# Last perceptron's second product by a seven-product scheme in groups 0 to 2, with weight sums made by adding transfers

## The reference, cut to what matters

```python
def sqrelu_mlp(h, w1, w2):
    a = jax.nn.relu(h @ w1)
    return (a * a) @ w2
```

## Time and profile before

| | us |
|---|---|
| runs, median of 3 | 2924.24 |
| runs, lowest and highest | 2922.78, 2925.26 |
| profiled execution, span from first to last instruction | 2926.7 |
| of it TensorE busy | 2837.7 |
| VectorE busy | 1374.1 |
| ScalarE busy | 1144.5 |
| GpSimd busy | 1320.1 |

### The profile page before, as it was taken

How to read it: one execution, slowest core, us unless ns; L and a number is a source line. 1 busy time by engine, 2 the same in 40 slices (tenths; PEclk the granted TensorE clock), 3 DMA queues, 4 the chain that set the end, 5 groups by cost and what they waited for, 6 DMA issues and landing times.

```text
span 2926.7 us, 41107 instructions
## 1 busy us (share of the span) xinstructions
PE 2837.7 (97%) x16278; PEld 2342.1 (80%) x16278; DVE 1374.1 (47%) x2568; ACT 1144.5 (39%) x1955; POOL 1320.1 (45%) x851
## 2 busy tenths in 40 slices
PE   7789999999999999989999999999999999999999
PEld 7577778888888786778888787888878878888887
DVE  4448653141121476632111467776543468667432
ACT  4353554453332443543322444332433543323332
POOL 4253247874444441344444553344534633435344
PEclk9999999999999999999999999999999999999999
DMA  6834114553223324032333332111222421212223
GB/s 242 318 113 142 51 44 146 180 165 100 94 94 130 110 82 156 1 108 87 96 99 94 111 113 70 58 58 58 87 72 87 137 88 47 66 58 73 87 72 115
DMA packets 84862, 300.69 MB, mean 103 GB/s; under 512 B 9536, under 2 KB 9920, under 8 KB 84288
## 3 DMA queue, kind: packets, MB, share of 16 engines
q1 hardware_dynamic: 84672, 298.07, 31.5%
HBM read 295.94 MB, written 2.10 MB: 102 GB/s over the span
## 4 chain that ended last, share of the span: by engine, by line
PE 84%; DVE 10%; ACT 2%; issue 2%; DMA 1%; POOL 1%; SPq 0%; POOLq 0%; ACTq 0%; DVEq 0%
PE ps L639 65%; PE ps L612 5%; DVE ps L2438 4%; PE ps L814 3%; PE ps L835 2%; PE ps L667 1%; PE ps L1011 1%; PE ps L1074 1%; PE ps L1085 1%; PE ps L939 1%; DMA t<-in_wmod 1%; PE ps L1252 1%; DVE t L2738 1%; DVE t L2776 1%; PE ps L952 0%
## 5 line engine op out<-in xcount | busy, mean ns | idle before, releaser
L639 PE MATMUL ps<-t,t 128*128 128x512 f32 (+3 forms) x9936 | 2218.6, 381 | 22.0 <-DVE t L2140 7.3
L639 PEld LDWEIGHTS ps<-t,t 128*128 128x128 f32 x9936 | 1781.0, 189 | 368.7 <-issue 35.5
L3087 POOL TENSOR_TENSOR t<-t,t 128x1024 fp32r<-128x1024 f32 (+3 forms) x464 | 1082.3, 2337 | 1078.8 <-ACT t L1397 1040.3
L1397 ACT ACTIVATE t<-t 128x1024 fp32r<-128x1024 f32 (+3 forms) x464 | 476.5, 1031 | 840.8 <-PE ps L639 784.9
L612 PE MATMUL ps<-t,t 128*128 128x128 f32 (+2 forms) x1662 | 238.4, 278 | 25.8 <-DVE t L2347 3.9
L612 PEld LDWEIGHTS ps<-t,t 128*128 128x128 f32 (+2 forms) x1662 | 190.1, 141 | 72.8 <-ACT t L1546 16.6
L2541 DVE TENSOR_TENSOR ps<-ps,t 128x512 f32<-128x512 f32 (+1 forms) x96 | 57.3, 606 | 343.7 <-ACT t L1739 343.7
L2558 DVE TENSOR_TENSOR t<-ps,t 128x512 f32<-128x512 f32 x56 | 38.2, 692 | 201.0 <-PE ps L639 200.9
L2438 DVE SCALAR_TENSOR_TENSOR ps<-t,t,ps 128x512 f32<-128x512 f32 (+1 forms) x174 | 116.1, 667 | 6.4 <-ACT ps L1654 0.6
L3107 POOL TENSOR_TENSOR t<-t,t 128x4 f32<-128x4 f32 (+2 forms) x96 | 86.4, 900 | 59.8 <-DVE t L2144 27.4
L814 PE MATMUL ps<-t,t 96*128 96x384 f32 (+1 forms) x320 | 104.6, 449 | 4.8 <-DVE t L2301 2.4
(11 more groups left out here) (279 smaller groups left out, 2480.3 us busy)
## 6 DMA issues: line engine op xcount, KB each, us to landing
t<-in_wbig SPq DMA_DIRECT2D x424, 512.0 KB, 3.5
t<-in_wmod SPq DMA_DIRECT2D x96, 512.0 KB, 6.6
t<-in_wbig SPq DMA_DIRECT2D x16, 416.0 KB, 3.1
t<-in_wbig SPq DMA_DIRECT2D x16, 332.0 KB, 2.9
t<-in_wbig SPq DMA_DIRECT2D x14, 256.0 KB, 2.6
t<-in_wbig SPq DMA_DIRECT2D x6, 384.0 KB, 3.1
t<-in_x SPq DMA_DIRECT2D x1, 2048.0 KB, 7.7
out<-t SPq DMA_DIRECT2D x8, 256.0 KB, 4.4
```

The lines of the kernel that those rows point to most:

```text
L639: m = p.matmul(out, lhs, rhs, start=kk == 0 and n == 0, stop=kk == tiles - 1 and n == 2)
L1397: a.activation(c.hi(w), c.raw(w), ACT.Copy).then_inc(w_hi.h, w_hi.up(("cut", w)))
L3087: g.tensor_tensor(c.lo(w), c.raw(w), c.hi(w).bitcast(F32), ALU.subtract).then_inc(w_lo.h, w_lo.up(("cut", w)))
```

## The change

In groups 0 to 2 of "ml1" the second product is made by seven products of quarter size in place of eight. Let the hidden activations of a group be a 2 x 2 of blocks A (256 tokens by 512 hidden columns) and w2's part a 2 x 2 of blocks W (512 by 512). The seven products are named 11, T3, 21, T4, T1, T2 and 22, in this order. Each has two units of 12 matmuls: two weight tiles, two banks of 128 tokens, three matmuls. T4, T2 and 22 accumulate in the banks of T3, 11 and T1, after VectorE has added those to Y.

Three of the weight operands are blocks of w2 (11, 21, 22). The other four are sums of two or three blocks. SyncE loads the first block of each into a buffer of its own (WN, 1 MB, `fetch_first`). GpSimd then issues five transfers that add into these buffers (`add`, `accum_op`): T3 += 22, T1 += 11, T4 += 22, T2 += T3 and T4 += T1, the last two from SBUF. They are issued in the first "w1" stage of a group (in group 0 in the second), behind GpSimd's cut of its unit 0 (one), unit 1 (two) and unit 2 (two).

The squares of the relu are kept in full in a buffer HF, with no split of their own. VectorE makes the four block sums of them (`full`) and all low parts (`low`); ScalarE makes the high parts (`part`). Of the 14 weight units of a group VectorE makes the low part where `by_vector` says so, GpSimd of the rest. VectorE adds each finished product to the places of Y that it belongs to (`took`, nine operations of 128x1024 in a group). Of the second output half, -Y is kept up to group 2, so group 3 subtracts. The row of gains moves behind product T1 of group 0.

The diff, cut to its core:

```diff
        "kc": [(3592, 4104)], "vc": [(4104, 4616)], "zc": [(4616, 5128)]}
+WN = ("11", "T3", "21", "T4", "T1", "T2", "22")
+WN_BLOCKS = ("11", "21", "22", "12")
+WN_SUM = {"T3": ("12", "22"), "T1": ("12", "11"), "T4": ("21", "22", "T1"), "T2": ("11", "T3")}
+WN_ADD = (("T3", 1), ("T1", 1), ("T4", 1), ("T2", 1), ("T4", 2))
+WN_PAIR = {"11": 0, "T3": 1, "21": 2, "T4": 1, "T1": 3, "T2": 0, "22": 3}
+WN_ONTO = {"T4": "T3", "T2": "11", "22": "T1"}
+WN_PART = {"11": 0, "T3": 1, "21": 2, "T4": 3, "T1": 0, "T2": 1, "22": 2}
 LAYER = {"c0": 0, "l0": 0, "c1": 1, "l1": 1, "mc0": 0, "ml0": 0, "ml1": 1}
+
+
+def seven(n, g):
+
+    return n == "ml1" and g < 3
 
...
                     block(("w1", n, g, h), "w_mlp_in", (i,), row, 4, [(1024 * g + 512 * h, 1024 * g + 512 * h + 512)])
+            if seven(n, g):
+                for name in WN_BLOCKS:
+                    row, col = 1024 * g + 512 * (int(name[0]) - 1), 512 * (int(name[1]) - 1)
+                    block(("wn", n, g, name), "w_mlp_out", (i,), row, 4, [(col, col + 512)])
+                continue
...
+    def wn_from(self, x):
+
+        return self.WN[x[1]][x[3]][:, x[4], :]
...
+    def by_vector(self, x):
+
+        if isinstance(x, tuple):
+            return x[4] == 1
+        key = self.units[x][0]
+        return key[0] == "wn" and key[3] != "11" and self.of[key].index(x) == 1
+
+    def seven_units(self, n, g, name):
+
+        return [("wn", n, g, name, r) for r in range(2)] if name in WN_SUM else self.of[("wn", n, g, name)]
...
+        self.WN, self.HF = {}, {}
+        w, a = self.row(one, [[128, 2, 1024]] * 3)
+        self.WN["ml1"] = dict(zip(WN_SUM, [*w, self.XC]))
+        self.HF["ml1"], _ = self.row(self.top - 16384, [[128, 4, 512]] * 2)
+
...
+        def seven_products(g):
+            for name in WN_SUM:
+                c.use(("r", (n, g, name)))
+            for name in WN:
+                at, onto = pairs[WN_PAIR[name]], WN_ONTO.get(name)
+                if onto:
+                    P.wait_ge(dve, ("took", n, g, onto))
+                else:
+                    for m in (at, at + 1):
+                        opened(m, ((dve, ("took", n, g, {0: "T2", 1: "T4", 2: "21", 3: "22"}[WN_PAIR[name]])),))
+                c.where[("wn", n, g, name)] = at
+                P.wait_ge(act, ("parth", n, g, name))
+                P.wait_ge(dve, ("partl", n, g, name))
+                aH, aL = c.wn_part(n, name)
+                for r, x in enumerate(c.seven_units(n, g, name)):
+                    c.use(("p" if name in WN_SUM else "w", x))
+                    hi, lo = (w.rearrange("p (k n) -> p k n", k=2) for w in (c.hi(x), c.lo(x)))
+                    P.wait_ge(w_hi, ("cut", x))
+                    P.wait_ge(dve if c.by_vector(x) else w_lo, ("cut", x))
+                    for k in range(2):
+                        for b in range(2):
+                            for m_, (wp, ap) in enumerate(((hi, aH), (hi, aL), (lo, aH))):
+                                m = p.matmul(c.BK[at + b], ap[:, 2 * r + k, 128 * b:128 * b + 128], wp[:, k, :],
+                                             start=not onto and r == k == m_ == 0, stop=r == k == 1 and m_ == 2,
+                                             skip_group_check=bool(onto))
+                        if k:
+                            m.then_inc(gemm.h, gemm.up(("w", x), *([("product", n, g, name)] if r else [])))
+                        yield
+                if (g, name) == (0, "T1"):
+                    row_of(n, i, 1, int(n[1] == "c"), pairs[2])
+            pairs[0:3] = pairs[2], pairs[1], pairs[0]
+
         for g in range(4):
...
+        while upto[0] < len(c.cut) and c.spos[c.cut[upto[0]]] <= c.spos[u] + ahead:
             w = c.cut[upto[0]]
             upto[0] += 1
             if c.before_in_slot(w) is not None:
                 A.wait_ge(gemm, ("w", c.before_in_slot(w)))
+            if isinstance(w, tuple):
+                A.wait_ge(c.s_sum[w[3]], ("sum", *w[1:4]))
+                a.activation(c.hi(w), c.wn_from(w), ACT.Copy).then_inc(w_hi.h, w_hi.up(("cut", w)))
+                continue
...
+        def part(g, name):
+            if name in ("11", "21", "T4"):
+                for kk in range(4 * int(name != "11"), 4 * int(name != "11") + 4):
+                    A.wait_ge(dve, ("hf", n, g, kk))
+            else:
+                A.wait_ge(dve, ("full", n, g, name))
+            if name in ("T1", "T2", "22"):
+                A.wait_ge(gemm, ("product", n, g, {"T1": "11", "T2": "T3", "22": "21"}[name]))
+            elif g:
+                A.wait_ge(gemm, ("product", n, g - 1, {"11": "T1", "T3": "T2", "21": "22", "T4": "T4"}[name]))
+            a.activation(c.wn_part(n, name)[0], c.wn_full(n, name), ACT.Copy).then_inc(
+                act.h, act.up(("parth", n, g, name)))
+
+        def first_parts(g):
+            yield
+            for name in ("11", "T3"):
+                part(g, name)
+                yield
+
+        def seven_products(g):
+            at = {0: ("21", "T4"), 2: ("T1",), 4: ("T2",), 6: ("22",)}
+            for m, x in enumerate(x for name in WN for x in c.seven_units(n, g, name)):
+                cut(x)
+                for name in at.get(m, ()):
+                    part(g, name)
+                if (g, m) == (0, 11):
+                    row_of(n)
+                yield
+                yield
+
         for g in range(4):
             for h in range(2):
-                main = product_gemm(("w1", n, g, h), 4, 8, lambda b: relu(g, h, b))
...
+        def low(g, name):
+            V.wait_ge(act, ("parth", n, g, name))
+            hi, lo = c.wn_part(n, name)
+            v.tensor_tensor(lo, c.wn_full(n, name), hi.bitcast(F32), ALU.subtract).then_inc(
+                dve.h, dve.up(("partl", n, g, name)))
+
+        def full(g, name):
+            F0, F1 = c.HF[n]
+            A11, A21, A12, A22 = F0[:, :, 0:256], F0[:, :, 256:512], F1[:, :, 0:256], F1[:, :, 256:512]
+            V.wait_ge(dve, dve.n)
+            out, one, other, op = {"T3": (A12, A11, A21, ALU.subtract), "T1": (A21, A21, A22, ALU.subtract),
+                                   "T2": (A11, A21, A11, ALU.subtract), "22": (A12, A12, A11, ALU.add)}[name]
+            v.tensor_tensor(out, one, other, op).then_inc(dve.h, dve.up(("full", n, g, name)))
...
+        def seven_products(g):
+            low(g, "21")
+            low(g, "T4")
+            cut(g, "T3")
+            yield from steps(4)
+            full(g, "T1")
+            full(g, "T2")
+            took(g, "11")
+            cut(g, "21")
+            yield from steps(4)
+            low(g, "T1")
+            full(g, "22")
+            took(g, "T3")
+            yield from steps(4)
+            low(g, "T2")
+            cut(g, "T4")
+            took(g, "21")
+            yield from steps(4)
+            low(g, "22")
+            cut(g, "T1")
+            took(g, "T4")
+            yield from steps(4)
+            cut(g, "T2")
+            took(g, "T1")
+            cut(g, "22")
+            yield from steps(4)
+            took(g, "T2")
+            yield from steps(4)
+            took(g, "22")
...
-        while upto[0] < len(c.cut) and c.pos[c.cut[upto[0]]] <= c.pos[u] + ahead:
+        while upto[0] < len(c.cut) and c.spos[c.cut[upto[0]]] <= c.spos[u] + ahead:
             w = c.cut[upto[0]]
             upto[0] += 1
+            if c.by_vector(w):
+                continue
+            if isinstance(w, tuple):
+                G.wait_ge(w_hi, ("cut", w))
+                g.tensor_tensor(c.lo(w), c.wn_from(w), c.hi(w).bitcast(F32), ALU.subtract).then_inc(
+                    w_lo.h, w_lo.up(("cut", w)))
+                continue
             G.wait_ge(w_hi, ("cut", w))
             G.wait_ge(c.s_of(w), ("raw", w))
...
+        def add(gr, name, step):
+            block = WN_SUM[name][step]
+            if step == 1:
+                G.wait_ge(c.s_wn[name], ("first", n, gr, name))
+            else:
+                G.wait_ge(c.s_sum[name], ("added", n, gr, name, step - 1))
+            if block in WN_SUM:
+                G.wait_ge(c.s_sum[block], ("sum", n, gr, block))
+                source = c.WN[n][block][:, :, :]
+            else:
+                source = c.wn_block(n, gr, block)
+            done = ("sum", n, gr, name) if step == len(WN_SUM[name]) - 1 else ("added", n, gr, name, step)
+            g.dma_start(c.WN[n][name][:, :, :], source, accum_op=ALU.add).then_inc(
+                c.s_sum[name].h, c.s_sum[name].landed(done))
+
+        def adds(gr):
+            for name, step in WN_ADD:
+                yield
+                yield
+                add(gr, name, step)
+
         for gr in range(4):
...
+    def fetch_first(n, g, name):
+        if g == 0:
+            S.wait_ge(dve, ("x", "l1", 3))
+            S.wait_ge(act, ("ss", "c1", 1))
+            S.wait_ge(turned, ("pt", "c1", 7))
+        else:
+            old = ("wn", n, g - 1, name, 1)
+            S.wait_ge(w_hi, ("cut", old))
```

(53 more changed lines are left out.)

101 lines of the change are left out of this document (84 added, 17 removed).

## The result

The changed kernel took 2941.84 us, median of four runs (2939.43 to 2946.32), against 2923.99 for the kernel before: ratio 1.0062, 95% interval 1.0048 to 1.0076. It is 18 us slower where 7.5 us less was forecast, and outside the range.

A forecast was written before the change was run, and what follows sets the result against it. TensorE, busy 97% of the span, was taken to bound the kernel. Matmuls removed 16.3, minus turns 6.3, minus additions 2.5, made 7.5 us faster: 2916.7 against 2924.24 us; range 2908 to just past 2934.

The forecast's parts named there:

- What is removed: In the second product of groups 0 to 2: 24 matmuls less per group, 72 x 0.2267 = 16.3 us saved.
- The adding transfers: GpSimd's five 1 MB transfers a group: 6.3 us each to land, costing 2.5 us in group 0, nothing in groups 1 and 2.
- Rival D: Additions take 9.5 us each, so weight sums and cuts come late: 20 us lost to them, 2934; chance 0.22.
- Its sign for group 0: TensorE would wait in group 0 on ScalarE's cut of a sum, which waits for a transfer.
- two signs of being wrong altogether: Waits of TensorE in the first product, or a lower clock, would show the whole forecast wrong; no size given.
- The turns: In the product stage VectorE and GpSimd alternate on SBUF, VectorE keeping its turn: 2.1 us lost a group, 6.3 in three.
- B's case: GpSimd gets in where VectorE waits for its own last result: 14.4 us lost, 0.9 gained overall, 2923; chance 0.27.
- B's schedule: Product-stage waits if GpSimd gets in: 1.0 us at 21's second unit, 3.1 at T4, 0.7 at T4's second: 4.8 a group.
- The contention exists: In the product stage, VectorE operations with two SBUF inputs and GpSimd's SBUF reads make each other wait; 6.3 us taken.
- the row of gains: In group 0 it moves behind T1 with the same eight small matmuls: costs nothing.
- The contention of plain transfers: DMA share rises from 0.31 to some 0.6; costed at nothing, as raw weights have some 9 us of cover.

The follow-up runs named there:

- group 0 earlier: Changed kernel with additions further apart, VectorE's product stage reordered, group 0's first blocks all loaded at its first stage's start, its additions moved: 2910.90 us, ratio 0.9950.

## Why the prediction was wrong, by its own steps

**What is removed** held: 72 matmuls, 16.3 us; with the additions of group 0 away all of it came out in the time, and with group 0 earlier all of it shows in the trace.

**The adding transfers** is the step that failed first: a term of 2.5 us in the sum, for landings of 6.3 us each, with 7.7 as the upper end, reasoned from twice the bytes. They landed in 10.2 to 18.7, and the term was 13.8 us of waits, with 6.4 us of lower clock behind them. The engines' time was about as reasoned: 2.7% of the span for 15 is 5.3 us each, against 3.2 for a plain one of the same size (32.2% for 307.51 MB). The rule of the Trainium skill, "Collectives: The Full Stack", section The bandwidth ceiling, is that the second source read halves the rate; the trace goes that way, but not as far, 1.7 times the engines' time. The bound left out what lies between issue and landing, and no plain transfer of before showed it. How much of that is the addition itself and how much its company is open: in the profiles of the changed kernel and of its mended versions the DMA engines were 0.93 busy and more over the 8 us that began 1.2 us behind an issue, and no run has an addition alone. I priced the mechanism itself (the fifth waits for the third, the cuts queue behind it) as nothing in groups 1 and 2 and 2.5 us in group 0. It was 3.1 + 3.1 + 7.6 us of waits. Rival D named it, with its threshold of 8.5 us and 2 to 5 us in groups 1 and 2; its 2934 lacked the clock. (Its 12 us late in group 0 do not follow from its own times, 20.8 and 12.8, which are 8 apart.) Its sign for group 0 was another, though: a wait for ScalarE's cut of a sum, where it was GpSimd's cut of a raw unit, held up behind the issue. The prediction's two signs of being wrong altogether, waits in the first product (the stages "w1") and a lower clock, both came.

**The turns.** I took 2.1 us a group, from VectorE keeping its turn over two operations in a row. That was one instance, and it was misread. GpSimd's row at 1663.22 has "[1.29 <-DVE t L2253]": it stood idle until line 2253 of VectorE was through, and the code says why. GpSimd's program has a wait for just that result at this place (line 3160 of the kernel before):

```python
    def residual_pair(j):
        G.wait_ge(dve, ("rmean", "ml1", j))
        root(c.rs[:, 8 + 2 * j:10 + 2 * j], ("rr", "ml1", j))
        yield
        if j == 0:
            G.wait_ge(dve, ("x", "ml1", 1))
```

So the order of the program held GpSimd back, and no row showed a kept turn. The changed kernel shows who gets in: GpSimd, at the end of the operation that runs. That is B's case, left as a rival for want of a row. B's schedule had 1.0, 3.1 and 0.7 us at 21, T4 and T4's second unit; measured 0.84, 2.64 and 0 in groups 1 and 2, so 7.0 us of waits in all, with 3.5 us of lower clock behind those at T4. In group 0 they did not come, behind its longer wait.

**The clock** was missing from the sum: behind each wait of 2.6 to 7.6 us 1.7 to 2.9 us were lost to the lower clock, 10.0 us in all. Every wait was priced at its length alone. For the additions and the turns together the sum took off 8.8 us; in the trace they cost 31.8, of it some 21 by the additions and 11 by the turns.

Right: the contention exists and is worth a loss; the schedule with B's rule gave each wait its place; the row of gains cost nothing. The contention of plain transfers, costed at nothing, made no wait of TensorE in groups 1 and 2, but once the rest was mended, raw units of group 0 landed up to 16 us later than usual.

## What to carry to other kernels

An engine that issues transfers which wait for each other holds all its other work behind these waits: issue each where its predecessor has surely landed, not where the queue has room. Here landings took up to 18.7 us, and 16 us and more between the two were enough in groups 1 and 2. When work is moved to VectorE beside GpSimd, add up both engines' operations that read two tiles in SBUF as if they were one engine, and order them by what TensorE wants first. Before an idle stretch is put down to contention, look in the program for a wait that explains it. A wait of TensorE of a few microseconds can cost more than its length; where a change trades matmuls for work with little slack, a single such wait eats what tens of matmuls gave.

## What the runs showed of the hardware

- 1 MB added into SBUF from GpSimd's queue, with others in flight, lands in 10.2 to 18.7 us (median 12.5) in the changed kernel and in 8.6 to 18.3 in the fastest version with all sums (group 0 earlier), 5.7 for a plain 1 MB from SyncE; issuing one takes GpSimd 1.2 us from HBM and 0.88 from SBUF.
- Behind 13 of 17 waits of TensorE between 2.5 and 3.7 us the granted clock fell (0.50 to 0.74 over the next 3 us), behind the other four it stayed at 1.00. It fell behind the three longer waits (5.07 to 7.63 us), and behind none of 1.62 us and less.
- Between the two engines the turn went to GpSimd. It got in at the end of VectorE's running operation even where VectorE had its next one ready (at 1465.34): in no run here did a cut of 128x1024 on GpSimd take over 3.23 us for 2.39, a delay of less than one VectorE operation. Once in, it kept the turn over three cuts in a row, and a VectorE operation of 1.2 us took 6.6 us beside them, ending 1.1 us behind them:

```profile
1428.86 7.30 POOL L3338 TENSOR_TENSOR t<-t,t 128x1024 fp32r<-128x1024 f32 x3
...
1430.67 6.58 DVE L2738 TENSOR_TENSOR t<-t,t 128x1024 fp32r<-128x1024 f32 x1 [4.89 <-ACT t L1891]
```
